# Stick-breaking attention: differences taken on neighbouring rows of V instead of on neighbouring cumulative products

## What is computed

```
def stick_breaking_attention(q, k, v):           # per block of 128 queries
    z = (q @ k.T) * scale
    strict = key position < query position
    log_keep = where(strict, log_sigmoid(-z), 0)
    log_rest = reverse cumsum(log_keep) - log_keep
    a = where(strict, exp(log_sigmoid(z) + log_rest), 0)
    out = a @ v
```

## Time and profile before

| what | before |
|---|---|
| median of the runs | 3178.75 us |
| the profiled execution, its span | 3177.3 us |
| its instructions | 36092 |
| TensorE busy | 3005.1 us (95%) |
| VectorE busy | 1491.1 us (47%) |
| ScalarE busy | 724.1 us (23%) |
| GpSimd busy | 355.3 us (11%) |

### The profile page before, as it was taken

The page is one execution under the profiler, slowest core; times in us unless marked ns, Lnnn a source line. Parts: engine busy times, 40 slices in busy tenths (PEclk is TensorE's granted clock), DMA queues, the critical chain, the costliest instruction groups (busy, mean ns, idle before and its releaser), DMA issues.

```text
span 3177.3 us, 36092 instructions
## 1 busy us (share of the span) xinstructions
PE 3005.1 (95%) x14479; PEld 1659.0 (52%) x14479; DVE 1491.1 (47%) x2829; ACT 724.1 (23%) x1521; POOL 355.3 (11%) x218
## 2 busy tenths in 40 slices
PE   8999899998989899999999999999989887999998
PEld 5888443787744344446856533333345543444443
DVE  5994842998392434675575311211144753011112
ACT  1210542121262201111124201100015642111111
POOL 4553000655200000000001100000000000000000
PEclk9999999999999899999999899999999998999999
DMA  5452003456201222110412799999931003999997
GB/s 225 164 194 80 27 1 129 155 184 244 80 1 40 108 83 106 36 53 8 169 67 88 314 389 399 376 389 377 396 122 56 24 3 148 412 421 421 421 421 295
DMA packets 89896, 606.07 MB, mean 191 GB/s; under 512 B 10809, under 2 KB 11612, under 8 KB 19205
## 3 DMA queue, kind: packets, MB, share of 16 engines
q1 hardware_dynamic: 79776, 575.70, 45.4%
q0 software_dynamic: 4432, 15.73, 1.6%
q10 hardware_dynamic: 5524, 12.35, 1.2%
HBM read 592.73 MB, written 11.01 MB: 190 GB/s over the span
## 4 chain that ended last, share of the span: by engine, by line
PE 63%; DVE 7%; ACT 2%; issue 1%; another core or an unknown queue 0%; DVEq 0%; ACTq 0%; PEldq 0%
PE ps L1359 8%; PE ps L2763 7%; PE ps L2725 7%; PE ps L2776 4%; PE ps L2742 4%; PE ps L2806 4%; PE ps L1092 3%; PE ps L3056 2%; PE ps L2613 2%; PE ps L1457 2%; PE ps L2815 2%; PE ps L2529 2%; PE ps L2630 2%; PE ps L1697 2%; PE ps L3217 1%; PE ps L1509 1%
## 5 line engine op out<-in xcount | busy, mean ns | idle before, releaser
L611 PE MATMUL ps<-mem 128*128 128x256 f32 x1792 | 393.3, 381 | 13.2 <-DVE mem L641 10.8
L611 PEld LDWEIGHTS ps<-mem 128*128 128x128 f32 x1792 | 340.3, 191 | 65.5 <-DVE mem L641 14.4
L556 POOL TENSOR_TENSOR mem<-mem 128x512 f32<-128x512 f32 (+1 forms) x160 | 301.7, 1885 | 535.2 <-DVE mem L852 276.5
L754 DVE SCALAR_TENSOR_TENSOR mem<-mem 128x1024 f32<-128x1024 f32 x160 | 254.7, 1632 | 13.8 <-DMA mem<-in_ada_w 12.9
L1359 PE MATMUL ps<-mem 128*128 128x512 f32 (+1 forms) x768 | 254.7, 494 | 2.9 <-ACT mem L1200 2.9
L2763 PE MATMUL ps<-mem 128*64 128x512 f32 x1024 | 223.3, 594 | 0.0
L2725 PE MATMUL ps<-mem 128*64 128x512 f32 x1024 | 222.5, 592 | 0.7 <-ACT mem L2659 0.7
L1359 PEld LDWEIGHTS ps<-mem 128*128 128x128 f32 x768 | 147.5, 193 | 109.5 <-issue 98.3
L641 DVE TENSOR_TENSOR mem<-ps,mem 128x256 f32<-128x256 f32 x308 | 121.3, 418 | 111.9 <-PE ps L611 68.4
L1092 PE MATMUL ps<-mem 128*128 128x512 f32 x384 | 169.6, 597 | 1.8 <-DVEq L156 1.8
L2915 DVE TENSOR_TENSOR mem<-ps,mem 128x512 f32<-128x512 f32 x16 | 11.1, 691 | 314.1 <-PE ps L2725 314.1
(11 more groups left out here) (420 smaller groups left out, 4156.9 us busy)
## 6 DMA issues: line engine op xcount, KB each, us to landing
mem<-in_moe_w SPq DMA_DIRECT2D x384, 1024.0 KB, 13.9
mem<-in_w_in SPq DMA_DIRECT2D x48, 1024.0 KB, 8.1
mem<-in_ada_w SPq DMA_DIRECT2D x48, 1024.0 KB, 5.0
mem<-in_hy_w_in SPq DMA_DIRECT2D x24, 1024.0 KB, 6.9
mem<-in_w_out SPq DMA_DIRECT2D x12, 1024.0 KB, 6.0
mem<-in_k_win_l SPq DMA_DIRECT2D x8, 1024.0 KB, 6.9
mem<-in_hy_w_out SPq DMA_DIRECT2D x8, 1024.0 KB, 5.0
mem<-in_sw_w_in SPq DMA_DIRECT2D x6, 1024.0 KB, 7.1
```

The source lines that it names most:

```text
L556: gp(out, x, y, op).then_inc(A.mark(sem), 1)
L611: m = mm(seven(l, unit), x[:, k, :], y[:, k, :], start=(k == 0), stop=(k == 3))
L754: stt(PRODUCT if again else w, w, 1.0, C_ROWS[:, z, :], ALU.mult, ALU.mult, accum_out=mod(layer, b // KD, b % KD, z))\
```

## The change

The subtraction of each stick-breaking unit on VectorE is gone: the second scan of a unit now releases the transposes. ScalarE, when it copies the transposed products of kind 1 out of PSUM, adds -1 from a constant column (`Identity` with a bias in place of `Copy`). V of kind 1 is replaced once per layer, during the projection, by the difference of neighbouring keys. For this GpSimd clears one row at block 24; ScalarE, at j = 30, issues two DMAs that copy V one key further into `V_BEFORE`, which is the still unused `KT[:, 8:12, :]`; GpSimd at block 36 waits for both and then makes four subtractions of 128x512, ahead of the folds of block 36; and ScalarE at j = 36 waits for these four before it copies anything into the K tiles. Four new semaphore names share the numbers of existing ones.

```
+                if j == 24:
+                    nc.gpsimd.memset(V_BEFORE[0:1, 0, :], 0.0).then_inc(A.mark("v_moved"), 1)
+                if j == 36:
+                    A.e.wait_ge(S["v_moved"], 33)
+                    for i in range(NQ):
+                        made(VN[:, NQ + i, :], V_BEFORE[:, i, :], VN[:, NQ + i, :], ALU.subtract, "v_stepped")
...
+                if j == 30:
+                    A.e.wait_ge(S["product_read"], READ_NO[24, 6, 1])
+                    e.dma_start(V_BEFORE[1:P], VN[0:P - 1, NQ:2 * NQ, :]).then_inc(S["v_moved"], 16)
+                    e.dma_start(V_BEFORE[0:1, 1:NQ, :], VN[P - 1:P, NQ:2 * NQ - 1, :]).then_inc(S["v_moved"], 16)
+                if j == 36:
+                    A.e.wait_ge(S["v_stepped"], NQ)
...
+        V_BEFORE = KT[:, 8:12, :]
...
-                    act(dst, src, ACT.Copy).then_inc(A.mark("turned_out"), 1)
+                    if kind == 1:
+                        act(dst, src, ACT.Identity, bias=MISC[:, 3:4]).then_inc(A.mark("turned_out"), 1)
+                    else:
+                        act(dst, src, ACT.Copy).then_inc(A.mark("turned_out"), 1)
...
-            for pset in P_SETS:
-                nc.vector.memset(pset[:, :, 512:513], 1.0).then_inc(A.mark(), 1)
-            A.e.wait_ge(*A.last)
...
-                                .then_inc(A.mark(), 1)
-                        A.e.wait_ge(*A.last)
-                        tt(pset[:, :, 512 - kw:512], pset[:, :, 513 - kw:513], pset[:, :, 512 - kw:512], ALU.subtract)\
-                            .then_inc(A.mark("weights"), 1)
+                                .then_inc(A.mark("weights" if c else None), 1)
```

More of the change, by code:

```diff
@@ L184 @@
               "aux_full", "aux_act", "aux_dve", "sel_scaled", "pair_map", "ctx_map", "product", "inverted", "spread", "selected"]
+SHARED_SEMS = {"sums_made": "ctx_full", "v_moved": "ctx_out", "v_stepped": "ctx_turned", "masked": "ctx_silu"}
 def build(nc, a, out):
@@ L206, in build @@
                 sems[n] = ctx.enter_context(nc.semaphore(f"{n}_{turn}"))
-            nums = [x.num for x in sems.values()]
+            for n, other in SHARED_SEMS.items():
+                sems[n] = sems[other]
+            nums = sorted({x.num for x in sems.values()})
             assert max(nums) - min(nums) == len(nums) - 1
@@ L371, in dve_setup @@
             nc.vector.memset(MISC[:, 2:3], 0.0).then_inc(A.mark(), 1)
+            nc.vector.memset(MISC[:, 3:4], -1.0).then_inc(A.mark(), 1)
             for i, sem in enumerate(X_IN):
```

## The result

The changed kernel takes 3258.33 us (median of 4 runs, 3257.49 to 3259.56), the kernel before, run beside it, 3179.09 us. The ratio is 1.0249, 95% interval 1.0237 to 1.0261: 79 us slower. The profiled execution's span is 3255.3 us, 78.0 more than before. Names of lines have moved: the folds and subtractions of GpSimd are L562, the products of a block L623 (and L621 for V blocks), ScalarE's copies L640, VectorE's additions L653, the transposes L985, the products with V L1002.

What follows compares the result with a forecast made beforehand. VectorE bounds stick-breaking, TensorE the projection. Stalls of 32.9 and 43.7 us, plus 1.8, less 3.2, make 75.2 lost; 10.1 gained leaves 65.1 us slower: span 3242.4, median 3243.9 us, range 3196 to 3285.

Steps and rivals of the forecast that it cites:

- One DMA engine: Projection: the 127-row DMA that shifts V lies on one DMA engine and takes 39.8 us.
- Loads in turn: Projection: weight loads take turns with the shift on its engine, landing it 16.3 and 25.6 us later; chance 0.62.
- rival with free loads: Projection: one engine, but weight loads cost the shift nothing; 23.2 us slower, 3202.0 us; chance 0.19.
- the one with a copy at half rate: Projection: one engine, and a copy within SBUF runs at half a load's rate; 3323.5 us; chance 0.06.
- The first layer: First layer's projection: shift lands at 271.0, TensorE goes on at 279.0, having waited 32.9 us, plus 1.8 for restart.
- The second layer: Second layer's projection: shift lands at 813.2, TensorE goes on at 821.2, having waited 43.7 us, less 3.2 for an earlier pause.
- VectorE will have run dry: Projection, behind the landing: GpSimd's four subtractions and two folds take 1.34 us each, 8.0 together, with VectorE out of work.
- The attention: Stick-breaking stretch: without VectorE's subtraction TensorE becomes the limit; gain 5.05 us per layer, 10.1 us for two.
- `Identity` with a bias has the copy's shape and ScalarE has slack there: nothing: Attention, ScalarE's copies out of PSUM: adding -1 from a constant column costs no time.
- the predicted 8.35: Stick-breaking units: a pair takes 8.35 us of TensorE, from 9.45 for kind 2 less 1.10 for its bias.
- The rival of a spread shift: Projection: the shift spreads over 16 engines, lands before 220 and stays hidden; 3168.7 us, faster; chance 0.08.
- if GpSimd takes the gain back: Projection: spread shift, but GpSimd's subtractions make VectorE 3.7 us later per layer; 3176.0 us, no change; chance 0.05.

Runs made afterwards that it cites:

- two engines: The changed kernel with the long DMA cut into 122 and 5 rows in place of 127: 3214.6 us, ratio 1.0106 to the kernel before.
- attention-only kernel: The changed kernel with V neither moved nor subtracted, so its output is another: 3172.63 us, ratio 0.9977 to the kernel before.
- the one subtraction: Kernel with spread shift two blocks earlier, immediate -1, GpSimd subtracting ahead of block 32: one 128x2048 subtraction in place of four of 128x512; 3178.12 us.
- none on GpSimd: Kernel with spread shift two blocks earlier and immediate -1: VectorE makes one 128x2048 subtraction ahead of block 32, GpSimd none; 3173.8 us, ratio 0.9986.

## Why the prediction was right, and where it was off

- **One DMA engine.** Right, and it carries the result: 26 GB/s at 6.3% of the engines, 59 and 70 us to landing; cutting the rows in 112 + 15 takes about 70 of the 79 us away, two engines take 44. The rule read from 71 tiny packets is the one that the Trainium skill states ("DMA: Bandwidth & Descriptors", section on why a DMA increments its semaphore by 16), with 127 as its example; the trace now shows that example.
- **Loads in turn.** Right: 16.3 and 25.6 us were put down for them, 17.6 and 28.6 are left of the landing times, and the loads that really came in between make 17.7 and 28.1. With the short DMA first 22.3 and 31.3 are left where the loads make 18.5 and 27.7, so this holds to about 4 us. The rival with free loads falls with this, the one with a copy at half rate with the 26 GB/s.
- **The first layer.** The shift was to land at 271.0 and did by 272.5; TensorE was to go on at 279.0 and did at 280.8. Its loss was put at 34.7 us and is 34.8. The form was missed: 17 us of it are taken at block 32, where ScalarE stands at the second issue. The prediction counted what waits for the landing, not what stands behind the issue on ScalarE's own queue. The standing cost nothing more, since the landing ends last. That the size agrees this closely is luck in part: in the form that was predicted, one pause at block 36, the short DMA first loses 40.7 us.
- **The second layer.** 40.5 us were predicted, 48.1 measured. In the time of before, TensorE was to go on at 821.2; it did at 861.5 - 34.5 = 827.0. Of these 5.8 us the landing is 2.0. The four subtractions took 7.56 us where 5.36 were put down, 2.2 more, and the two folds behind them 861.5 - 857.5 = 4.0 in place of 2.7: "VectorE will have run dry" was wrong here. It had other work waiting (`ada_w` products, 1.23 and 2.28 us at 849.5 and 850.7), and none in the first layer, where VectorE was busy 0.00 us of the stretch and the four took 5.28. Of the other 1.8 us 1.1 is the restart: behind 861.5 the lag grows by another 2.9 us, where the prediction had 1.8. TensorE's granted clock shows why. After 21.22 us of idling it was 0.66 of full in the stretch below (the row's last three numbers are clock, DMA share, GB/s) and 1.00 from 870 to 887, so TensorE went on at the lower of its two levels (1.2 and 2.4 GHz) for a part of it. The last 0.7 arise later, between the projection and the stick-breaking units; their cause isn't shown.

```profile
861.52:870.00 8.48, 8.48 (x26) 6.94 (x27) 7.41 (x9) 0.00 (x0) 7.29 (x6) 0.66 0.01 2
```

- **The attention.** 10.1 us were predicted; 7.1 came in the stick-breaking units, and the kernel with this part alone is 7 to 8 us faster. That TensorE takes over as the limit is right. The failed step is "`Identity` with a bias has the copy's shape and ScalarE has slack there: nothing". An engine's slack over a stretch says nothing of one activation that TensorE waits for. It is 0.09 us longer with a constant column, which is 0.27 of the 0.42 us by which a pair is over the predicted 8.35. The other 0.15 is the size of what TensorE's own transposes take more: three rows of a stick-breaking pair take 0.88, 1.09 and 0.44 us with the immediate -1, the same rows of a pair of kind 2 before 0.83, 1.04 and 0.39. The 8.35 were worked out from such a pair of kind 2; why its transposes are shorter isn't shown. The Trainium skill gives about 93 ns for each such operand ("ScalarE: Activation LUTs", section "What ACT_TABLE_LOAD costs"); the measured 0.09 agrees.
- **Not foreseen:** 3.8 us at the start of the second layer, far from any edit. GpSimd's folds there fall otherwise against VectorE's products; it isn't in the traces of the attention-only kernel or of the one subtraction, but it is with none on GpSimd. Open.
- **The sum.** 65.1 us were predicted, 78.0 measured in the profiled executions: 7.6 more in the second layer, 3.8 at its start, 3.0 less gain and 0.1 in the first layer, less 1.6 given back behind the attention, make 12.9. Later stages took up hardly any of the loss, as the prediction had it.
- **The rival of a spread shift** gave 3168.7 us if hidden and 3176.0 if GpSimd takes the gain back. With the shift really spread it was 3188.9. Both left out that the shift, spread or not, is in the way of the weights that are in flight at its issue; moved out of their way, with the immediate -1 and the subtraction given to VectorE, it comes to 3173.8.

## What to carry to other kernels

Count the rows of a DMA before its bytes: 127 rows went over one engine at 26 GB/s, 112 + 15 of the same rows in 12 us, and on the slow engine the full sixteenth of every other load is added. An issue is work on its engine's queue, so look at what stands right behind it, and when a transfer competes with weights, move its issue to where the queue is idle. Idle time of GpSimd beside a busy VectorE is not free: an operation that is moved there may cost VectorE most of its own length (4.3 us for one of 4.96).

## What the runs showed of the hardware

- The issue of a second DMA stood for 21 to 24 us on ScalarE while a long one of 127 rows lay on one engine. With 61 rows on each of two engines, or with the short one first, the second issue took 0.6 to 1.2 us.
- A copy from SBUF to SBUF ran at 26 GB/s on one engine, the sixteenth of the 418 GB/s that loads reached on 16.
- A VectorE product that began inside a GpSimd operation of 128x2048 ended only 1.1 us after it (5.50 us for 1.22, and 5.51 in the second layer); four of 128x512 lengthened three products to 2.05 to 2.27 us each.
- An activation out of PSUM with a bias from a column took 0.09 us longer than with an immediate one at all four sizes from 128x256 to 128x1024; a scale from a column cost `Copy` of 128x512 as much.
- TensorE's granted clock was 0.66 over the first 8.5 us after a pause of 21.2 us, and 1.00 over the 17 us behind these.
